# Dilated attention mixed with dense k steps, head norms as columns, the masked block left out

## The reference

```
q = rms_norm(heads(pq), q_gain) * (HEAD_DIM ** -0.5)
k = rms_norm(heads(pk), k_gain)
s = einsum('bdnqhe,bdnkhe->bdnhqk', qb, kw)
s = where(valid, s, NEG_INF)
m = max(s); pexp = exp(s - m); den = sum(pexp)
o = (pexp / den) @ v;   lse = m + log(den)
alpha = softmax(lse over the three groups);  out = o * alpha
merged = g_a * (y_a @ w_proj_rwkv) + g_b * (y_b @ w_proj_attn)
```

## Time and profile before

| | us |
|---|---|
| median of 3 runs | 3818.41 (3813.82 to 3821.29) |
| the profiled execution | 3813.28 |
| its span | 3811.4 |
| TensorE busy | 3546.8 (93%), 15308 instructions |
| VectorE busy | 816.2 (21%) |
| ScalarE busy | 538.8 (14%) |
| mean granted clock of TensorE | 0.954 |

### The profile page before, as it was taken

One profiled execution on the slowest core, in us unless ns is written; L12 is line 12 of the kernel. 1 busy time (PEld: TensorE's weight loads), 2 busy tenths in 40 slices (PEclk: granted clock), 3 DMA queues, 4 the chain that ended last, 5 costly groups with the idle time before them and its releaser, 6 DMA issues.

```text
span 3811.4 us, 35451 instructions
## 1 busy us (share of the span) xinstructions
PE 3546.8 (93%) x15308; PEld 2270.4 (60%) x15308; DVE 816.2 (21%) x1506; ACT 538.8 (14%) x1040; POOL 0.2 (0%) x4
## 2 busy tenths in 40 slices
PE   8999999799998988999799998999979899899998
PEld 6877687587873444444444443444434585477787
DVE  1012631531002044110730011000030421430101
ACT  1002321121002011000510101000021110311100
POOL 0000000000000000000000000000000000000000
PEclk9999799879998999999899999999989999999999
DMA  4344433324344110121011113121212133122332
GB/s 183 135 144 152 155 135 112 110 102 177 140 158 154 66 44 22 66 88 66 23 45 66 44 66 127 72 76 58 76 66 88 45 111 111 45 102 99 130 140 102
DMA packets 27501, 371.95 MB, mean 98 GB/s; under 512 B 3040, under 2 KB 3168, under 8 KB 3296
## 3 DMA queue, kind: packets, MB, share of 16 engines
q1 hardware_dynamic: 27216, 368.85, 26.3%
q10 hardware_dynamic: 144, 1.05, 0.1%
HBM read 368.84 MB, written 1.05 MB: 97 GB/s over the span
## 4 chain that ended last, share of the span: by engine, by line
PE 87%; DVE 9%; ACT 2%; issue 1%; DMA 0%; DVEq 0%; SPq 0%; ACTq 0%
PE bank L515 87%; DVE small L2134 1%; PE bank L518 1%; DVE merged_T L2072 1%; DVE merged_T L2086 1%; DVE arena L1928 1%; DVE arena L1604 0%; DVE arena L2106 0%; DVE h_T L1610 0%; DVE arena L1906 0%; DVE arena L2144 0%; DVE arena L2145 0%; DVE arena L2066 0%; DVE h_T L1631 0%; ACT L1223 0%
## 5 line engine op out<-in xcount | busy, mean ns | idle before, releaser
L515 PE MATMUL bank<-h_T,weights 128*128 128x256 f32 (+1 forms) x5744 | 1692.0, 457 | 41.3 <-DVE h_T L1610 16.8
L515 PEld LDWEIGHTS bank<-h_T,weights 128*128 128x128 f32 x5744 | 1104.6, 193 | 623.9 <-issue 483.4
L515 PE MATMUL bank<-arena,weights 128*128 128x256 f32 (+2 forms) x2464 | 706.8, 451 | 13.5 <-DVE small L1688 4.5
L515 PEld LDWEIGHTS bank<-arena,weights 128*128 128x128 f32 (+1 forms) x2464 | 467.9, 193 | 249.4 <-issue 186.9
L515 PE MATMUL bank<-weights,h_T 128*128 128x512 f32 (+1 forms) x768 | 323.9, 583 | 0.0
L515 PEld LDWEIGHTS bank<-weights,h_T 128*128 128x128 f32 x768 | 145.9, 190 | 175.8 <-issue 167.4
L515 PE MATMUL bank<-arena 64*64 64x64 f32 (+7 forms) x1616 | 223.0, 338 | 24.2 <-DVE arena L1930 8.6
L1650 DVE TENSOR_TENSOR arena<-arena,bank 128x256 f32 (+3 forms) x88 | 42.9, 487 | 728.1 <-PE bank L515 728.1
L515 PEld LDWEIGHTS bank<-arena 64*64 64x64 f32 (+2 forms) x1616 | 152.0, 179 | 65.8 <-issue 30.3
L1269 ACT ACTIVATE arena<-bank 128x256 f32<-128x256 f32 (+1 forms) x88 | 38.5, 437 | 664.3 <-PE bank L515 664.2
L515 PE MATMUL bank<-arena,merged_T 128*128 128x257 f32 (+1 forms) x528 | 86.7, 332 | 36.5 <-DVE merged_T L2086 19.5
(11 more groups left out here) (235 smaller groups left out, 1623.9 us busy)
## 6 DMA issues: line engine op xcount, KB each, us to landing
weights<-wide_slabs_dram SPq DMA_DIRECT2D x151, 2048.0 KB, 7.7
weights<-down_slabs_dram SPq DMA_DIRECT2D x32, 1408.0 KB, 5.8
masks<-second_consts_dram SPq DMA_DIRECT2D x1, 2240.0 KB, 8.8
masks<-first_consts_dram SPq DMA_DIRECT2D x1, 1120.0 KB, 7.5
x_T<-x_T_dram SPq DMA_DIRECT2D x1, 1024.0 KB, 4.9
merged_T<-ctx_T_dram SPq DMA_DIRECT2D x1, 1024.0 KB, 10.9
out_dram<-h_T ACTq DMA_DIRECT2D x1, 1024.0 KB, 3.9
params<-params_dram SPq DMA_DIRECT2D x1, 287.5 KB, 5.3
```

Of the source, the lines that this page charges most:

```text
L515: return mm(out, lhsT, rhs, start=start, stop=stop, skip_group_check=True)
```

## The change

Four things are done at once.

- **The head norms become columns.** The squares of q and k are now the stationary side, 128 tokens at a time, against two columns of `pair`; the sums of all 24 head halves and both query halves stand in one bank as 128x48, tokens as rows. Root and reciprocal are taken on 48 columns. The query factor is not multiplied into q: it is a column `DIL_R`, applied together with the mask when the scores are read (`stt`, L1994). The key factor is spread over 64 rows by 24 matmuls (`DIL_R` as a broadcast stationary column against the identity) and multiplied into k with both gains, three products of 128x512 (L1971).
- **The block that is always masked is left out**: the first 128 queries see only the first 128 keys. A head has 384 score columns instead of 512, three transposes instead of four, three value matmuls instead of four, and the mask table is 1152 columns instead of 1536.
- **Dense k steps go into the loop.** `dil_fill` issues single matmuls of `rwkv_proj1` and `dil_gate0` (8 tiles, 64 matmuls) into banks 2 and 3: 8 before the loop, then 5 in each iteration until none is left (in h = 11). VectorE empties the first four tiles between heads (`proj1_out`), ScalarE copies the other four, and their sigmoids come after the loop's small chain.
- **ScalarE squares q and k earlier**, right after their copies and ahead of the roots of the group norm.

```diff
@@ -212,7 +212,8 @@
...
-C1_N = 704 + 1536
+C1_N = 704 + 1152
+DIL_KEYS = ((0, P), (P, 3 * P))
@@ -464,12 +465,20 @@
...
         def DIL_P(h):
-            return A[:, 10752 + (h % 3) * 512:10752 + (h % 3) * 512 + 512].rearrange("p (q k) -> p q k", q=2)
+            return A[:, 10752 + (h % 3) * 512:10752 + (h % 3) * 512 + 3 * P]
...
         def DIL_PT(h):
-            return A[:, 12288 + (h % 2) * 512:12288 + (h % 2) * 512 + 512]
+            return A[:, 12288 + (h % 2) * 512:12288 + (h % 2) * 512 + 3 * P]
...
+        DIL_SUM, DIL_R = small[:, 48:96], small[:, 96:144]
+        DIL_GAIN = small[:, 144:145]
+        DIL_FILL0, DIL_FILL = 8, 5
+        def dil_filled(h):
+            first = lambda n: max(0, (DIL_FILL0 + DIL_FILL * n) // KT)
+            return range(first(h), min(8, first(h + 1)))
...
         def DA_PT(n):
@@ -962,20 +971,51 @@
...
-            branch_projections("rwkv", slot3(sR), act_frees("dil_v", 2))
+            sq = tiles(A, 7680, 12, T)
+            t.wait("act_for_pe")
+            t.wait("dve_for_pe")
+            for q in range(2):
+                for k in range(12):
+                    n = 24 * q + 2 * k
+                    last = matmul(bank[4][:, n:n + 2], sq[:, k, q * P:(q + 1) * P], pair[:, 0:P:64])
+            last.then_inc(S["pe_for_dve"], 1)
+            yw = slot3(sR)
+            project(ST["rwkv_proj0"], lambda k: yw[:, k], T, drains=by_dve, frees=act_frees("dil_v", 2))
+            t.wait("dve_for_pe")
+            for k in range(6):
+                for q in range(2):
+                    n = 24 * q + 12 + 2 * k
+                    cols = (k % 2) * T + q * P
+                    for g in range(2):
+                        rows = slice(64 * g, 64 * g + 64)
+                        last = matmul(bank[5 + k // 2][rows, cols:cols + P], DIL_R[:, n + g:n + g + 1].to_broadcast([P, 64]), ident)
+            last.then_inc(S["pe_for_dve"], 1)
+            dense = [0]
+            def dil_fill(count):
+                st0, st1, g0 = ST["rwkv_proj0"], ST["rwkv_proj1"], ST["dil_gate0"]
+                for _ in range(count):
+                    tile, k = divmod(dense[0], KT)
+                    if tile == 8:
+                        return
+                    dense[0] += 1
+                    st = st1 if tile < 4 else g0
+                    if k == 0:
+                        arrived(st, 0)
+                        if tile < 2:
+                            pe.wait_ge(S["dve_out"], st0.dve0 + tile + 3)
+                        elif tile < 6:
+                            pe.wait_ge(S["dve_out"], st1.dve0 + tile - 1)
+                        else:
+                            pe.wait_ge(S["act_out"], g0.act0 + tile - 5)
+                    rhs = yw[:, k] if tile < 4 else H1[:, k]
+                    last = matmul(bank[2 + tile % 2][:, 0:T], wtile(st, 0, (tile % 4) * KT + k), rhs, start=k == 0, stop=k == KT - 1)
+                    if k == KT - 1:
+                        last.then_inc(S["tile_done"], 1)
...
-            for half in range(2):
-                if half == 0:
-                    t.wait("act_for_pe")
-                else:
-                    t.wait("dve_for_pe")
-                for b in range(3):
-                    src = A[:, 7680 + (3 * half + b) * 512:7680 + (3 * half + b + 1) * 512]
-                    last = matmul(bank[4 + b][:, :], pair, src)
-                last.then_inc(S["pe_for_dve"], 1)
-                gate("dil", 0, dve_frees("rwkv_proj1"), part=(2 * half, 2 * half + 2))
+            dil_fill(DIL_FILL0)
@@ -983,38 +1023,38 @@
...
-                for q in range(2):
-                    last = matmul(bank[h % 2][:, q * T:(q + 1) * T], qk[rows, h // 2, q * P:(q + 1) * P], qk[rows, 6 + h // 2])
+                for q, (lo, hi) in enumerate(DIL_KEYS):
+                    last = matmul(bank[h % 2][:, lo:hi], qk[rows, h // 2, q * P:(q + 1) * P], qk[rows, 6 + h // 2, 0:hi - lo])
...
             def dil_turn(h):
...
-                for q in range(2):
-                    for k in range(2):
-                        last = transpose(bank[4 + h % 2][:, (2 * q + k) * P:(2 * q + k + 1) * P], DIL_P(h)[:, q, k * P:(k + 1) * P])
+                for n in range(3):
+                    last = transpose(bank[4 + h % 2][:, n * P:(n + 1) * P], DIL_P(h)[:, n * P:(n + 1) * P])
...
             def dil_values(h):
-                pt = DIL_PT(h).rearrange("p (q k) -> p q k", q=2)
+                pt = DIL_PT(h)
...
-                    for k in range(2):
-                        last = matmul(bank[6 + h % 2][:, q * 64:(q + 1) * 64], pt[:, q, k * P:(k + 1) * P], v1[:, k, h * 64:(h + 1) * 64],
-                                      start=k == 0, stop=k == 1)
+                    for k in range(q + 1):
+                        last = matmul(bank[6 + h % 2][:, q * 64:(q + 1) * 64], pt[:, (q + k) * P:(q + k + 1) * P], v1[:, k, h * 64:(h + 1) * 64],
+                                      start=k == 0, stop=k == q)
...
             for h in range(15):
...
+                dil_fill(DIL_FILL)
...
-            gate("dil", 1, act_frees("dil_gate0"))
+            gate("dil", 1, [("act_out", ST["dil_gate0"].act_end)])
@@ -1449,23 +1489,23 @@
...
+            act.wait_ge(S["act_out"], st.act_end)
+            t.out(af(A[:, 7680:10752], A[:, 3072:6144], ACT.Square), "act_for_pe")
...
-            t.out(af(A[:, 7680:10752], A[:, 3072:6144], ACT.Square), "act_for_pe")
-            for half in range(2):
-                t.wait("dve_for_act")
-                t.out(af(A[:, 15360:16896], A[:, 15360:16896], ACT.Sqrt), "act_for_dve")
-                gate("dil", 0, tiles(A, DIL_GATES, KT, T), 8, part=(2 * half, 2 * half + 2))
+            t.wait("dve_for_act")
+            t.out(af(DIL_SUM, DIL_SUM, ACT.Sqrt), "act_for_dve")
+            dil_gates = tiles(A, DIL_GATES, KT, T)
...
-                    for q in range(2):
-                        ins = af(DIL_P(h)[:, q], DIL_P(h)[:, q], ACT.Exp, bias=stat[:, 24 + 2 * h + q:25 + 2 * h + q],
+                    for q, (lo, hi) in enumerate(DIL_KEYS):
+                        ins = af(DIL_P(h)[:, lo:hi], DIL_P(h)[:, lo:hi], ACT.Exp, bias=stat[:, 24 + 2 * h + q:25 + 2 * h + q],
@@ -1475,11 +1515,22 @@
...
-                    t.out(af(DIL_PT(h), bank[4 + h % 2][:, :], ACT.Copy), "pt_ready")
+                    t.out(af(DIL_PT(h), bank[4 + h % 2][:, 0:3 * P], ACT.Copy), "pt_ready")
+                for tile in dil_filled(n):
+                    if tile >= 4:
+                        st = ST["dil_gate0"]
+                        act.wait_ge(S["tile_done"], st.done0 + tile - 3)
+                        af(dil_gates[:, tile - 4], bank[2 + tile % 2][:, 0:T], ACT.Copy).then_inc(S["act_out"], 1)
...
-            gate("dil", 1, tiles(A, DIL_GATES, KT, T), 8)
+            act.wait_ge(S["act_out"], ST["dil_gate0"].act_end)
+            for c in range(4):
+                ins = af(dil_gates[:, c], dil_gates[:, c], ACT.Sigmoid, bias=pc("b_gate", 8 + c))
+                if c < 3:
+                    t.step(ins)
+            t.out(ins, "act_for_dve")
+            gate("dil", 1, dil_gates, 8)
@@ -1908,42 +1959,53 @@
...
-            merge("rwkv", G1, T, True, gates=G1)
-            for half in range(2):
-                t.wait("pe_for_dve")
-                for b in range(3):
-                    dst = A[:, 15360 + b * 512:15360 + (b + 1) * 512]
-                    if half == 0:
-                        ins = ts(dst, bank[4 + b][:, :], 1.0, 64 * EPS, mul, add)
-                    else:
-                        ins = ts(dst, bank[4 + b][:, :], 1.0 / 64, EPS, mul, add)
-                    if b < 2:
-                        t.step(ins)
-                t.out(ins, "dve_for_act")
-                t.wait("act_for_dve")
-                rs = A[:, 15360:16896]
-                t.step(nc.vector.reciprocal(rs, rs))
-                qkf = A[:, 3072 + half * 1536:3072 + (half + 1) * 1536]
-                t.out(stt(qkf, qkf, pc("q_norm" if half == 0 else "k_norm"), rs, mul, mul), "dve_for_pe")
+            t.wait("pe_for_dve")
+            t.out(ts(DIL_SUM, bank[4][:, 0:48], 1.0, 64 * EPS, mul, add), "dve_for_act")
+            t.step(stt(DIL_GAIN, pc("q_norm"), 8.0, pc("k_norm"), mul, mul))
+            t.wait("act_for_dve")
+            t.out(nc.vector.reciprocal(DIL_R, DIL_SUM), "dve_for_pe")
+            merge("rwkv", G1, T, True, gates=G1, halves=(0,))
+            t.wait("pe_for_dve")
+            for b in range(3):
+                kf = A[:, 4608 + b * 512:4608 + (b + 1) * 512]
+                ins = stt(kf, kf, DIL_GAIN, bank[5 + b][:, :], mul, mul)
+                if b < 2:
+                    t.step(ins)
+            t.out(ins, "dve_for_pe")
+            def proj1_out(tile):
+                st = ST["rwkv_proj1"]
+                dve.wait_ge(S["tile_done"], st.done0 + tile + 1)
+                tt(G1[:, 4 + tile], G1[:, 4 + tile], bank[2 + tile % 2][:, 0:T], mul).then_inc(S["dve_out"], 1)
+                dve.wait_ge(S["dve_out"], st.dve0 + tile + 1)
...
```

(17 more changed lines are left out.)

7 lines of the change are left out of this document (4 added, 3 removed).

## The result

| | before | changed |
|---|---|---|
| median, us | 3816.11 (4 runs, 3812.67 to 3821.29) | 3771.66 (4 runs, 3767.95 to 3774.80) |
| ratio, 95% interval | | 0.9883 (0.9871 to 0.9894) |
| profiled execution | 3813.28 | 3767.95 |
| its span | 3811.4 | 3766.2 |
| mean granted clock | 0.954 | 0.962 |

The changed kernel is faster by 44.5 us, 1.2%; 3776 was forecast, with a core of 3769 to 3785 and outer cases at 3763 and 3796. From the page of the changed kernel: the span, the engines, the chain that ended last, and the load of the mask table (KB, us to landing).

The account below looks back on a forecast made before the run. TensorE was taken as the bound, at half clock in the loop. Seven terms sum to 100.3 us instead of 142.3; with 0.4 for the start, 3770.9 profiled, 3776 us median, with 62% on 3769 to 3785.

Parts of the forecast that it names:

- wait for the group norm's product: Before the sums: ScalarE's earlier squaring delays VectorE's chain by 0.65 us, so TensorE's wait of 3.4 us becomes 4.1.
- 48 two-column instructions: Sums of squares after the wait: 6.2 us at full clock or 11.2 at half; 10.5 us taken.
- first rwkv slab: First half of the rwkv projection, before the loop: 13.8 us plus half of about 4.8 lost while the clock returns, 16.2.
- spread factors: Before the loop, 24 matmuls spread reciprocals over 64 rows: upper bound 5.8 us, half if neighbouring halves run together; 3.0 taken.
- dense tile: Just before the loop: 16 dense instructions, 3.45 us, hiding three VectorE products of 128x512 that take 2.2 us with gaps.
- loop: Attention loop at full clock, 3.9 us per full iteration, idle time only in the tail: 47.3 us.
- second gate slab: Gate projection behind the loop: 13.8 us plus 2.0 because it starts at half clock, 15.8.
- earlier start: Kernel start: mask table 192 KB smaller, so it starts between 0 and 1.3 us earlier; 0.4 taken.
- Clock never falls around the loop: Rival, 10%: the clock never falls before or behind the loop, giving back 4.3 + 2.4 + 2.0 us: 3767.
- Bound by latency: Rival, 16%: latency or clock dips bind the loop, 5.1 us per iteration instead of 3.9, +11 us: 3787.
- Loop at half clock: Rival, 8%: the lower clock outlasts the loop's dense groups of 2.15 us, +43 us: 3819, no change.
- Slower: Rival, 4%: half clock lasts from the two-column instructions to the dense part behind the loop, some 28 us more doubled: 3847.

Follow-up runs that it names:

- experiment 1: Changed kernel with all 64 dense matmuls of the second rwkv slab and first gate ahead of the loop, none in it: 3797.25 us, ratio 0.9939.
- experiment 5: Changed kernel with one extra, unused VectorE reciprocal of 128x1536 ahead of the products of k, so TensorE waits before the loop: 3779.16 us, ratio 0.9896.
- 8: Changed kernel with four dense matmuls per head and the 24 sums in two groups of 12, around the value projection's last tile: 3761.13 us.
- 9: Changed kernel with four dense matmuls per head and the sums woven singly into the value projection's last two tiles: 3759.85 us, ratio 0.9842.
- Experiment 4: Changed kernel with squares back behind the roots and the 24 two-column sums ahead of TensorE's wait for the group norm's product: 3762.43 us, ratio 0.9852.
- 2: Changed kernel with the always masked block computed as before, four transposes and four value matmuls per head, full mask table: 3781.61 us, ratio 0.9906.
- 10: The changed kernel itself measured once more, nothing edited: 3773.39 us, ratio 0.9882.
- experiment 3: Kernel before with only the always masked block left out; norms, order and waits stay: 3802.24 us, ratio 0.9959.
- 7: Changed kernel with the sums ahead of the group norm wait and four dense matmuls per head instead of five: 3760.19 us, ratio 0.9849.
- 11: The kernel of 7 once more, beside the changed kernel on one chip: 3763.43 us, ratio 0.9851.

## Why the prediction was right, and where its terms were off

| step | forecast | profile |
|---|---|---|
| wait for the group norm's product | 4.1 | 4.25 |
| 48 two-column instructions | 10.5 | 10.2 |
| first rwkv slab | 16.2 | 16.6 |
| spread factors | 3.0 | 2.8 |
| dense tile | 3.45 | 3.65 |
| loop | 47.3 | 51.0 |
| second gate slab | 15.8 | 13.9 |
| sum | 100.3 | 102.4 |
| earlier start | 0.4 | 1.2 |

**The mechanism held.** That the loop would rise to full clock and stay there was the term on which 43 us hung. Experiments 1 and 5 show it, with the fill as its cause, not the removed wait; the prediction had given both reasons, the 3.45 us of dense work ahead and the 2.15 of every 3.9 us inside, and only the second is needed. The two long waits are gone, and no wait above 2 us stands between 688 us and the loop, but the columns cost something in their place. Beside the dense work at its full-clock price, some 28 us stood ahead of the loop before (683.5 to 753.0) and some 20 now (683.9 to 721.5). By this estimate from the windows the norms brought 7 to 8 us of the gain; no run takes them alone.

**The sums** came out at the half-clock price, taken from the group at 456.20. Experiments 8 and 9 show the other price: 0.108 us each at full clock against 10.2/48 = 0.213 here. The Trainium skill (TensorE: Matmul & The Clock Gate, LDWEIGHTS) gives a load of 128 columns as an estimate of 0.107 us; the runs agree with that at full clock, and at half clock they show twice as much. The prediction had named the longer wait and the lack of dense work behind it together. Experiment 4 took the wait away and the clock fell all the same, 3.3 us into the sums: a closed group of them brings it down without a wait, and the wait only makes it come sooner.

**The spread factors** came out at the lower bound. The 48 half-width instructions took 2.84 us, 0.06 each, half of the 0.12 of the full-width ones. The reason that the prediction gave, that neighbouring halves run side by side, is not shown by it: the weight loads, of 64 columns instead of 128, fill 2.60 of the 2.80 us by themselves, and that they are half as long would explain the same number. No run separates the two.

**The loop** was mis-sized by 3.7 us (the terms of its forecast add up to 47.2, not 47.3). The iteration is 4.15 us, not 3.9: four score instructions take 0.85 and not 0.67, five dense matmuls 2.26 and not 2.15. Over the eight full iterations (heads 3 to 10) these are 2.0 us, and the first three heads took 3.2, 3.2 and 3.5 us, 1.1 more in all. The dense figure came from the earlier trace rows, 0.215 per instruction in an unbroken stretch; between other shapes ten took 2.26. The tail took 7.0 and not 6.5, of which 1.83 us are the idle time that the prediction had put at 1.7. VectorE had 25.7 of 51.0 us and ScalarE 23.2, so neither was the bound, as expected.

**The gate behind the loop** was forecast at half clock at first, and in the changed kernel's profile it was not: 1.9 us less. In experiments 2, 4, 5 and 10 it was. The step was right as a likelihood and wrong for this execution; it covered half of the loop's error.

**The rest.** The stretch gave 39.9 us, 2.1 less than the 42.0 of the sum, but the spans differ by 45.2. The other 5.3 lie outside it. At the start 1.2 us were gained (ScalarE's second table load at 16.29 instead of 17.52 us, behind a mask load of 928 KB in 7.0 us instead of 1120 in 7.5), but they were lost again: the stage starts at 659.70 us, before at 659.29. A group of 64 instructions of 64x64 at 594.31, which the change doesn't touch, took 3.54 us at a clock of 0.53, where the kernel before had run it in 2.08 at 1.00. Behind the stage the same instruction is 39.5 us earlier at 3063.23 us (3023.77 changed), and 45.2 at 3799.16. Of these 5.7 us, 3.0 are one projection, here before and then changed:

```profile
3085.52 17.08 PE L515 MATMUL bank<-h_T,weights 128*128 128x256 f32 x64 [1.63 <-DVE arena L2106]
3046.06 14.08 PE L524 MATMUL bank<-h_T,weights 128*128 128x256 f32 x64 [1.64 <-DVE arena L2169]
```

Its mean clock was 0.82 before and 1.00 changed, behind the same wait. Differences of this size are met between like kernels: outside the stage, the profiled execution of experiment 3 gained 4.1 us less than its stage, that of 10 gained 11.5 more. Nothing in the traces ties them to the change. That the measured time came 4.3 us below the forecast is therefore luck: 2.3 of them are the lower median of the kernel before (3816.11 against 3818.41), and the saving was 2.1 larger than forecast although the changed stretch gave less, because the unchanged code, in these two executions, more than made up for it.

**The rivals.** *Clock never falls around the loop*: half true in the profile shown, behind the loop but not before it. *Bound by latency*: only at the tail. *Loop at half clock*: did not come for this kernel, but experiment 1 is its picture, 3.72 us a head. *Slower*: not seen; the clock was back within the first rwkv slab, 16.6 us long in the changed kernel, in each run.

## What to carry to other kernels

If a loop of small matmuls runs at half clock with TensorE busy throughout, look for dense matmuls that can be woven in, a few in every iteration; the same matmuls put in a block ahead of it don't help. Weave narrow matmuls evenly among dense ones too: the closed groups of 24 and 48 two-column instructions lowered the clock in each profile in which it stood at full in front of them (4, 7, 8 and 11), if not for themselves then for what stood behind them, and in the one profile where they were woven in (9) it held. And price each edit at the clock that will hold once the others are in: the left-out block was worth 1.06 us a head at half clock and 0.54 at full.

## What the runs showed of the hardware

- The granted clock can fall without any idle time. In experiments 4, 7 and 11 it stood at 1.00 and fell to 0.50 inside a group of two-column matmuls, in 8 within 1 us behind one, each time with TensorE counted busy throughout. In experiment 1 it fell in the first heads of the loop, with TensorE busy for 3.28 of 5.9 us, and did not return over 41 us of small matmuls (busy for 37.5), nor over 56 us before (54.3). The Trainium skill (TensorE: Matmul & The Clock Gate, Part 1: The HAM clock gate) ties the lower clock to an idle or cold TensorE; "busy" in the profile is thus not the activity that keeps the clock.
- In the loops with 2.26 of every 4.15 us in dense matmuls, and with 1.83 of 3.72, the clock stayed up, and in experiment 5 it came back 4.3 us after the loop's start.
- A wait of 3.4 us kept the clock at 1.00 in the kernel before and lost it in experiment 3 (mean 0.84), in front of the same instructions.
- A matmul of 2 columns behind a load of 128 costs 0.108 us at full clock and 0.213 at half.
- Half-width matmuls (64 stationary columns, 128 moving) that alternate between the lower and the upper half of the array ran at 0.06 us each, at full clock.
- A reciprocal of 128x48 on VectorE took 0.45 us, one of 128x1536 took 9.75.
